# Half gate products over all 64 heads, eight steps of a bound one stage earlier, and the two norms around the second block rebuilt

## What is computed

```python
x = rms_norm(x_first, final_g)                    # x_first: the first block's rows
h = _rms(x, norm1_g_2)
u, q, k, v, qi, ki, wi, gates = split(h @ w_in_2)
y_ssm = s5(u); y_ssm = y_ssm * sigmoid(y_ssm @ w_glu + b_glu)     # gated unit
iscore = sum_h relu(qi_h . ki) * wi_h             # causal; 4 index heads
idx = top_k(iscore, 256)                          # per query row
y_att = softmax(q . k over idx) @ v               # 8 heads of 64, 8 blocks of 128 queries
merged = sigmoid(g_ssm) * (y_ssm @ w_proj_ssm) + sigmoid(g_att) * (y_att @ w_proj_attn)
x = x + merged @ w_out
h2 = _rms(x, norm2_g_2)
x = x + (silu(h2 @ w_gate) * (h2 @ w_up)) @ w_down
```

## Time and profile before

| | us |
|---|---|
| median of 3 runs | 3938.29 |
| lowest, highest | 3937.95, 3939.74 |
| the profiled execution | 3939.54 |
| its span in the profile | 3937.70 |

### The profile page before, as it was taken

How to read it: one execution, slowest core, us unless ns; L and a number is a source line. 1 busy time by engine, 2 the same in 40 slices (tenths; PEclk the granted TensorE clock), 3 DMA queues, 4 the chain that set the end, 5 groups by cost and what they waited for, 6 DMA issues and landing times. The chain is left out here.

```text
span 3937.7 us, 32752 instructions
## 1 busy us (share of the span) xinstructions
PE 3623.9 (92%) x12692; PEld 1910.6 (49%) x12692; DVE 1520.3 (39%) x2703; ACT 759.4 (19%) x1408; POOL 368.3 (9%) x347
## 2 busy tenths in 40 slices
PE   7998999987889499999987999889999899999999
PEld 3445656544765344444433664345544444444444
DVE  3526662576333400001008563978521322222420
ACT  2004451442431000000002223223220111111000
POOL 0000000014620000000001020000000122221000
PEclk8999998988989699999988999889999999999999
DMA  6400000014332598888844032112132111110300
GB/s 241 142 9 23 1 1 14 30 58 120 87 124 96 176 347 311 316 318 322 309 154 186 0 64 83 51 30 75 33 112 96 43 43 43 43 50 30 144 22 32
DMA packets 200718, 431.22 MB, mean 110 GB/s; under 512 B 71561, under 2 KB 125993, under 8 KB 187761
## 3 DMA queue, kind: packets, MB, share of 16 engines
q1 hardware_dynamic: 191154, 397.85, 29.2%
q0 software_dynamic: 8272, 29.38, 2.5%
q10 hardware_dynamic: 1152, 2.10, 0.1%
HBM read 380.04 MB, written 48.07 MB: 109 GB/s over the span
## 5 line engine op out<-in xcount | busy, mean ns | idle before, releaser
L1820 PE MATMUL psum<-arena 128*128 128x512 f32 x1536 | 673.1, 596 | 5.5 <-DMA arena<-in_w_gate_dram 3.1
L3165 PE MATMUL psum<-arena 128*128 128x512 f32 x1232 | 531.5, 594 | 5.7 <-DVE arena L3223 4.1
L1820 PEld LDWEIGHTS psum<-arena 128*128 128x128 f32 x1536 | 290.4, 191 | 365.5 <-issue 362.5
L3165 PEld LDWEIGHTS psum<-arena 128*128 128x128 f32 x1232 | 234.4, 191 | 302.2 <-issue 294.5
L3319 PE MATMUL psum<-arena 128*128 128x512 f32 x528 | 228.6, 595 | 3.6 <-PEq L3138 3.6
L2809 PE MATMUL psum<-arena 128*128 128x512 f32 x416 | 201.7, 629 | 0.1
L742 PE MATMUL psum<-arena 128*128 128x512 f32 (+1 forms) x512 | 198.2, 543 | 1.1 <-PEq L456 1.1
L2897 DVE TENSOR_SCALAR_CACHE_REDUCE arena<-arena 128x1024 f32<-128x1024 f32 (+2 forms) x192 | 173.7, 943 | 1.9
L477 PE MATMUL psum<-arena 64*128 64x512 f32 (+1 forms) x384 | 156.1, 551 | 11.1 <-ACT arena L531 10.2
L3319 PEld LDWEIGHTS psum<-arena 128*128 128x128 f32 x528 | 100.3, 190 | 132.0 <-issue 131.8
L2113 PE MATMUL psum<-arena 128*128 128x512 f32 (+1 forms) x384 | 162.1, 582 | 0.0
(11 more groups left out here) (514 smaller groups left out, 4674.2 us busy)
## 6 DMA issues: line engine op xcount, KB each, us to landing
arena<-in_w_gate_dram SPq DMA_DIRECT2D x32, 2048.0 KB, 7.4
arena<-in_w_up_dram SPq DMA_DIRECT2D x32, 2048.0 KB, 9.1
arena<-in_w_down_dram SPq DMA_DIRECT2D x32, 2048.0 KB, 8.0
arena<-in_w_mod_dram SPq DMA_DIRECT2D x12, 2048.0 KB, 9.5
arena<-gd_rows SPq DMA_DIRECT2D x56, 256.0 KB, 4.3
arena<-in_w_in_dram SPq DMA_DIRECT2D x22, 512.0 KB, 4.3
arena<-in_w_ffn_gate_dram SPq DMA_DIRECT2D x11, 1024.0 KB, 5.4
arena<-in_w_ffn_up_dram SPq DMA_DIRECT2D x11, 1024.0 KB, 5.4
```

The costliest lines, as they stand in the source:

```text
L1820: ins = nc.tensor.matmul(ps[:, banks + j, :], lhs[:, k], W[n][:, h, k % 4, j * 512:(j + 1) * 512], start=(k == 0), stop=(k == KD - 1))
L3165: ins = nc.tensor.matmul(out(q), left[:, k], right[:, k], start=first and k == 0, stop=last and k == 3, skip_group_check=not first)
```

## The change

- *Experts' stage.* `final_g` and `norm1_g_2` are both broadcast into rows of `e.rows` that are no longer used, and GpSimd, after its first two gathers, makes from them the product of the two gains and the square of the final gain.
- *Between the blocks.* GpSimd has no work. ScalarE squares a tile, keeping the squares (`x2`) and their sum; VectorE multiplies them by the squared gain and sums (`tensor_tensor_reduce`). The factors take six small steps. One scaling by the product of the gains gives `xn`; the residual rows are neither computed nor stored, and only their factors are kept (`e.r3`). All copies of the turned rows are ScalarE's, in an order written out by hand. The gain is no longer loaded here.
- *Gated unit's stage.* Ahead of each of the eight products, VectorE does one of the first eight units of pair (7,6).
- *Sparse stage.* It starts that pair at unit 8 and spreads the 25 units left over heads 0 to 15. The 52 half gate products are spread over all 64 heads; ScalarE's copies go with them.
- *Output stage.* Two tiles in flight, in four banks; the other four banks take transpositions. Tile t-2 is turned right behind the products of tile t, and each tile has its own factor and root. VectorE makes the residual from `x_dram`, the kept factor and the final gain.

```diff
@@ stage_experts, SyncE and GpSimd
-            sp.dma_start(e.fgain, broadcast_rows(e.in_["final_g"])).then_inc(e.s_fgain, 16)
+            sp.dma_start(e.rows[:, 1], broadcast_rows(e.in_["final_g"])).then_inc(s_fgain, 16)
+            sp.dma_start(e.rows[:, 2], broadcast_rows(e.in_["norm1_g_2"][0])).then_inc(s_fgain, 16)
...
             gather(0)
             gather(1)
+            pool.wait_ge(s_fgain, 32)
+            nc.gpsimd.tensor_tensor(e.rows[:, 2], e.rows[:, 2], e.rows[:, 1], ALU.mult).then_inc(e.s_gains, 1)
+            pool.wait_ge(e.s_gains, 1)
+            nc.gpsimd.tensor_tensor(e.rows[:, 1], e.rows[:, 1], e.rows[:, 1], ALU.mult).then_inc(e.s_gains, 1)
@@ stage_between, ScalarE
+                nc.scalar.activation(x2[:, t % 4], x[:, t], ACT.Square, scale=D ** -0.5, accum_out=ss[:, 0, t:t + 1]).then_inc(s_sq, 1)
...
+            for t in range(4):
+                squares(t)
+            root(0)
+            squares(4)
+            turned(0)
+            turned(1)
+            root(1)
+            squares(5)
+            squares(6)
...
@@ stage_between, VectorE
+            dve.wait_ge(e.s_gains, 2)
+            sum_with_gain(0)
+            sum_with_gain(1)
+            for i in range(TL // 2):
+                spread(i)
+                if i < TL // 2 - 1:
+                    sum_with_gain(2 * i + 2)
+                scaled(2 * i)
+                scaled(2 * i + 1)
+                if i < TL // 2 - 1:
+                    sum_with_gain(2 * i + 3)
@@
+BOUND_UNITS, UNITS_GLU = 33, 8
+def bound_unit(nc, step, tiles, scores, u):
+    cand, drop, count, _, *junk = tiles
+    if u == 0:
+        step(nc.vector.memset(cand.bitcast(F32), 0.0))
+    for j, b in enumerate(scores):
+        ins = nc.vector.tensor_scalar(junk[j][:, 0:b.shape[-1]], b, cand.bitcast(F32)[:, j:j + 1], 0.0, ALU.is_ge, ALU.add, accum_out=count[:, j:j + 1])
...
@@ stage_glu, VectorE
-            outputs(0, 4)
+            for u in range(4):
+                bound_unit(nc, step, e.bound, widest, u)
+                outputs(u, u + 1)
             scores(0, NI)
-            outputs(4, 8)
+            for u in range(4, 8):
+                bound_unit(nc, step, e.bound, widest, u)
+                outputs(u, u + 1)
@@ stage_sparse
+    halves = lambda n: [divmod(k, 2) for k in range(2 * GN * n // len(heads), 2 * GN * (n + 1) // len(heads))]
...
-                if n // 2 < GN:
-                    gates(n // 2, n % 2)
+                for q, half in halves(n):
+                    gates(q, half)
...
-            r = 0
+            r = UNITS_GLU
...
+                upto = UNITS_GLU + (BOUND_UNITS - UNITS_GLU) * (n + 1) // (2 * HEADS) if a < 2 else BOUND_UNITS * (n + 1) // (2 * HEADS)
+                while r < min(upto, BOUND_UNITS * len(pairs)):
@@ stage_out2, TensorE
+                if t >= 2:
+                    pe.wait_ge(s_x4, t - 1)
...
+                if t >= 2:
+                    turn(t - 2)
+            turn(TL - 2)
+            turn(TL - 1)
@@ stage_out2, ScalarE
+            for t in range(TL):
+                squares(t)
+                root(t)
+                if t >= 2:
+                    turned(t - 2)
+            turned(TL - 2)
+            turned(TL - 1)
@@ stage_out2, VectorE
+                nc.vector.scalar_tensor_tensor(out=e.x4[:, t], in0=xr[:, t % 2], scalar=e.r3[:, t:t + 1], in1=g[:, 0], op0=ALU.mult, op1=ALU.mult).then_inc(s_x3, 1)
...
+            for t in range(TL):
+                residual(t)
+                spread(t)
+                modulated(t)
```

More of the change, by code:

```diff
@@ L1917, in _ @@
                 output(i, False)
-    A.give(*("w_" + n for n in names), "xe", "xT", "sg", "hid", "hidT", "y", "gcol", "rows", "idxT", "gateT")
+    A.give(*("w_" + n for n in names), "xe", "xT", "sg", "hid", "hidT", "y", "gcol", "idxT", "gateT")
 def stage_between(e):
@@ L1934, in stage_between @@
     vv = A.take("vv", 2, TL)
+    rr = e.scale1.rearrange("p a b -> p (a b)").rearrange("p (a b) -> p a b", b=TL)
+    e.r3 = rr[:, 0]
+    gain_sq, gains = e.rows[:, 1], e.rows[:, 2]
     s_x = [e.sem(f"bt_xin{i}") for i in range(TL)]
     e.w_p2, e.s_wp2 = A.take("w_p2", 3, KD, 512, high=True), [e.keep_sem(f"p2_w{i}") for i in range(3)]
-    s_in, s_own, s_sq, s_sg, s_xg, s_var, s_rt, s_x3, s_n, s_tr, s_ev, s_ev2 = (
-        e.sem(f"bt_{n}") for n in ("in", "own", "sq", "sg", "xg", "var", "rt", "x3", "n", "tr", "ev", "ev2"))
+    s_own, s_sq, s_s1, s_var, s_rt, s_n, s_tr, s_ev = (e.sem(f"bt_{n}") for n in ("own", "sq", "s1", "var", "rt", "n", "tr", "ev"))
     e.s_hst = e.keep_sem("bt_hst")
-    s_st = [e.sem(f"bt_st{i}") for i in range(TL)]
-    NP = TL // 2
     with nc.Block() as block:
@@ L2002, in _, with sum_with_gain, spread @@
             step = Steps(dve, s_own)
[L2003 to L2007, removed]
+            def sum_with_gain(t):
+                dve.wait_ge(s_sq, t + 1)
+                if t >= 2:
+                    dve.wait_ge(s_s1, t - 1)
+                nc.vector.tensor_tensor_reduce(out=junk[:, t % 2], in0=x2[:, t % 4], in1=gain_sq, scale=1.0, scalar=0.0, op0=ALU.mult, op1=ALU.add,
+                                               accum_out=ss[:, 1, t:t + 1]).then_inc(s_s1, 1)
+            def spread(i):
                 c = slice(2 * i, 2 * i + 2)
-                dve.wait_ge(s_sg, 2 * i + 2)
-                step(nc.vector.tensor_scalar(ss[:, :, c], ss[:, :, c], 1.0 / D, None, ALU.mult))
+                dve.wait_ge(s_s1, 2 * i + 2)
                 step(nc.vector.tensor_scalar(vv[:, 0, c], ss[:, 0, c], EPS, None, ALU.add))
@@ L2016, in _, with scaled @@
                 nc.vector.tensor_tensor(vv[:, 1, c], vv[:, 1, c], vv[:, 0, c], ALU.mult).then_inc(s_var, 1)
[L2017 to L2028, removed]
-                    turned(2 * i - 2)
-                    turned(2 * i - 1)
-            turned(TL - 2)
-            turned(TL - 1)
+            def scaled(t):
+                dve.wait_ge(s_rt, t // 2 + 1)
+                dve.wait_ge(s_x[t], 16)
+                if t >= 2:
+                    dve.wait_ge(s_tr, 2 * (t - 1))
+                nc.vector.scalar_tensor_tensor(out=xn[:, t % 2], in0=x[:, t], scalar=rr[:, 1, t:t + 1], in1=gains, op0=ALU.mult, op1=ALU.mult).then_inc(s_n, 1)
+            dve.wait_ge(e.s_gains, 2)
[9 more added lines that the diff above has]
+                    sum_with_gain(2 * i + 3)
         @block.tensor
@@ L2044, in _ @@
                         ins.then_inc(s_tr, 1)
-    A.give("x", "xn", "gain1", "final_gain", "junk", "ss", "xg", "vv")
+    A.give("x", "xn", "x2", "junk", "ss", "vv", "rows")
 TWO_PI = 2 * np.pi
@@ L2637, in stage_glu @@
     rel = A.take("rel", 2, 512)
+    cand, drop = A.take("cand", 2).bitcast(I32), A.take("drop", 2).bitcast(I32)
+    e.bound = (cand, drop, A.take("count", 2), A.take("room", 2), A.take("rank", L), A.take("equal", L))
+    widest = [B(i) for i in e.chosen[::-1][0:2]]
     QI, KI = 4, 7
@@ L2747, in stage_sparse @@
     B = lambda i: e.bias[i]
-    equal, rank = A.take("equal", L), A.take("rank", L)
-    cand = A.take("cand", 2).bitcast(I32)
-    bound, drop = cand.bitcast(F32), A.take("drop", 2).bitcast(I32)
-    count, room = A.take("count", 2), A.take("room", 2)
     e.w_proj, e.s_wproj = A.take("w_proj", 2, 4, D, high=True), [e.keep_sem(f"mg_p{i}") for i in range(2)]
@@ L2761, in stage_sparse @@
     turns = free + chosen[::-1]
-    pairs = [chosen[::-1][i:i + 2] for i in range(0, len(chosen), 2)]
+    pairs = [[B(i) for i in chosen[::-1][k:k + 2]] for k in range(0, len(chosen), 2)]
     s_own, s_sel, s_bias = (e.sem(f"sp_{n}") for n in ("own", "sel", "bias"))
@@ L2880, in _ @@
                     softmax(n)
-                if n >= 2 and n % 2 == 0 and n // 2 <= GN:
-                    gates((n - 2) // 2)
+                for q, half in halves(n - 1) if n else ():
+                    if half:
+                        gates(q)
                 if n > HEADS and n % HEADS == 2:
@@ L3037, in stage_out2 @@
     xr = A.take("x_ring", 2, D)
-    g = A.take("gain", D)
+    g = A.take("gain", 2, D)
     h = A.take("h", 2, D)
@@ L3042, in stage_out2 @@
     s_x = [e.sem(f"o2_xin{i}") for i in range(2)]
[L3043 removed]
+    s_g = [e.sem(f"o2_g{i}") for i in range(2)]
+    s_mm, s_x3, s_x4, s_sq, s_var, s_rt, s_own, s_h, s_tr, s_ev = (e.sem(f"o2_{n}") for n in ("mm", "x3", "x4", "sq", "var", "rt", "own", "h", "tr", "ev"))
     two = lambda v: v.rearrange("p (a n) -> p a n", a=2)
```

193 lines of the change are left out of this document (86 added, 107 removed).

## The result

| | before | changed |
|---|---|---|
| median, us | 3938.12 (6 runs, 3936.96 to 3940.26) | 3911.10 (6 runs, 3906.37 to 3915.55) |
| the profiled execution | 3939.54 | 3910.64 |
| its span | 3937.7 | 3908.8 |

The ratio is 0.9931, 95% interval 0.9918 to 0.9943: faster by 27 us. The forecast was 3909.4, and the sum against the profiled execution (-28.9) is what was measured (-28.9). That agreement is partly luck, as the windows of the changed kernel show at once (us, busy us of PE, PEld, DVE, ACT, POOL, then clock, DMA share, GB/s). They answer to the earlier trace rows.

A forecast was written before the change was run, and what follows sets the result against it. VectorE was taken to pace the sparse stage's first regime, TensorE its second, with a VectorE, ScalarE and GpSimd chain between the blocks; -13.4 + 1.5 - 12.8 - 4.2 = -28.9 gave 3909.4 us, range 3901 to 3918.

The forecast's parts named there:

- Part 1, first scaling, -9.7: Between the blocks: without GpSimd's work, the first scaling starts at 2073.1, not 2082.8, saving 9.7 us.
- pace, -2.1: Between the blocks: VectorE sets the pace at 6.2 us a pair; three pairs take 18.6, not 20.7, saving 2.1 us.
- tail, -1.6: Between the blocks: from the last pair's start to the next stage takes 6.0 us, not 7.6, saving 1.6 us.
- Part 1, experts, +1.5: Experts' stage: one more 512 KB broadcast ahead of the gate weights, which TensorE awaits, costs 1.5 us.
- Part 2, -22.4 + 0.2: Eight bound steps leaving the sparse stage's VectorE-paced regime save 22.4 us; in the gated unit's stage they cost 0.2.
- It can: Sparse stage, heads 0 to 15: TensorE can follow when head 16 starts 90.7 us after head 0, not 113.1.
- Part 3, net +9.4: Sparse stage: spreading the half products over 64 heads costs net 9.4 us, as three halves return where TensorE sets the pace.
- Heads 16 to 51: 7 x 3.43 = -24.0: Sparse stage: these heads have 29 half products in place of 36, each worth 3.43 us, saving 24.0 us.
- slower: the heads without a half product let the clock fall: Sparse stage rival: nine heads after head 15 without a half product cost 5.4 us each, giving 3958; chance 0.04.
- Clock over the shorter pause: Rival: TensorE's clock stays up before head 16, giving 3904; chance 0.12, shared with spreading being free.
- Part 4, -4.2: Output stage: transpositions between products cost 6 us, the tail falls from 17.1 to 6.9; net saving 4.2 us.
- The rule on transpositions: Output stage: if transpositions don't count as clock work, the next stage's first matmuls cost 3.7 us more, giving 3912.9.

The follow-up runs named there:

- pool_beside: Changed kernel with GpSimd doing eight products between the blocks again, into memory nobody reads: 3924.46 us, ratio 0.9969.
- sparse_only: Kernel before with only the bound's eight units in the gated unit's stage and half products over 64 heads; norms as before: 3934.39 us, ratio 0.9997.
- no_steps: Changed kernel with the bound's eight steps back in the sparse stage, 33 units over heads 0 to 15: 3928.73 us, ratio 0.9978.
- no_spread: Changed kernel with one half product on each of heads 0 to 51 and none behind: 3893.68 us, ratio 0.9897.
- norms_only: Kernel before with only both norms and the gains' products changed; sparse stage and gated unit's as before: 3909.13 us, ratio 0.9930.
- shifted: Changed kernel with the same spreading, its phase moved: heads without a half product are 2, 7, 12, 18, 23, 28, 34 and on: 3903.45 us, ratio 0.9914.

## Why the prediction was right, and where it was not

- **Part 1, first scaling, -9.7; pace, -2.1; tail, -1.6.** Right in place and size. From the load's issue to the first scaling it is 10.3 us, before 20.0; the three pairs take 17.5 (forecast 18.6, before 20.7); from the last pair on it is 5.7 (forecast 6.0). The sum is -15.0 for -13.4. The terms held the order of the chain and the slow steps together; pool_beside shows that work beside the chain is enough to undo nearly all of it.
- **Part 1, experts, +1.5.** Wrong: 0. TensorE's wait for the gate weights was 2.23 us, not 3.09 + 1.5; it was 0.64 to 2.48 in the other kernels with the broadcast and 2.49 in sparse_only, without it. That answers to the earlier trace rows. Of all traces only that of the kernel before has 3.09, and only its matmuls take 596 ns in the mean; this is the -5.5 of the table.
- **Part 2, -22.4 + 0.2.** The step that a unit costs 2.79 is right, and so is the cover in the gated unit's stage: a step and a product take 3.39 us there (2400.24 to 2403.63 in the changed kernel), with no wait of VectorE behind the first, which answers to the earlier trace rows. But by VectorE's lines, as in the earlier trace rows, head 16 starts 93.7 us after head 0 (2443.73 to 2537.40), not 90.7. The failed step is "It can", of TensorE: VectorE waited 3.51 us for it at head 8, where the kernel before has no such wait; the clock is 0.83 over that regime and a half product of 3.70 us takes up to 6.4. By the medians Part 2 is worth 17.6 and 15.4. With the spreading the sparse stage gives 17.4 of it (434.2 to 416.8). Without it that stage gives 20.1 (415.5 to 395.4), while the gated unit's goes from 46.6 to 50.1 at a lower clock (0.99 and 0.92); that isn't the steps' doing, since it takes 49.9 in no_steps, which has none there.
- **Part 3, net +9.4.** The mis-sized term, and the cause of the sparse stage's miss: +21.4. "Heads 16 to 51: 7 x 3.43 = -24.0" holds for five heads of the seven. For heads 16 and 32 it took for granted that TensorE is fast and sets the pace there. The rival *slower: the heads without a half product let the clock fall* had this mechanism and drew its line at six heads of nine; it came true at two, and at one of these, head 16, the clock was already down. The ten halves at the end cost 31.2 (33.1 forecast), and the merge behind them is shorter by 0.4 us (sparse_only against before) to 2.9 (changed against no_spread), a term the sum did not have.
- **Clock over the shorter pause.** The pause was 9.84 us (forecast some 10) and the clock fell, so that rival is out.
- **Part 4, -4.2.** -3.7, and -6.1 in norms_only. From the first product to the end of the last it is 116.0 us (110.1 + 6), and the tail is 7.5 (6.9) for 17.1. The same stage takes 121.1 to 123.6 us from trace to trace, so the half microsecond to the forecast says nothing.
- **The rule on transpositions.** Of the Trainium skill, "TensorE: Matmul & The Clock Gate", Part 4: PE-mode transpose, the forecast said that the trace disagrees. The rows of the changed kernel that answer to the earlier trace rows are:

```profile
3088.11 1.91 PE L3083 MATMUL psum<-arena 128*128 128x128 f32 x16
3092.78 1.90 PE L3083 MATMUL psum<-arena 128*128 128x128 f32 x8 [2.76 <-DVE arena L3148]
3095.62 7.43 PE L3207 MATMUL psum<-arena 128*128 128x512 f32 x12 [0.94 <-PEq L3057]
```

After a wait of 2.76 us the last eight transpositions run at 0.24 us each and the twelve records behind them at 0.62, so the clock was down, as that page's rule would have it, and as the wait alone would too: no run here parts the two. In no_spread the same wait is followed by fast transpositions, and only the products behind them are slow (the clock is 0.56 from 3075.10 to 3079.00):

```profile
3073.10 1.09 PE L3083 MATMUL psum<-arena 128*128 128x128 f32 x8 [2.76 <-DVE arena L3148]
3075.19 7.05 PE L3207 MATMUL psum<-arena 128*128 128x512 f32 x12 [0.99 <-PEq L3057]
```

Against the rule stands the kernel before: under transpositions alone its clock goes from 0.50 (3112.50 to 3114.50) to 1.00 (3116.00 to 3120.00). The fall in the changed kernel cost 0.8 us in the transpositions and none in the next stage, where the second large run of products starts 11.5 us after the first product in both kernels. The 3.7 us worked out from the rule were not there (and 3909.4 + 3.7 is 3913.1, not 3912.9).

Two of the forecast's own signs of being right did not come: head 16 started 93.7 us after head 0 and not 90 to 92, and from head 16 to the end the stage took 19.9 us longer, not some 9. One sign of being wrong did come, a wait of VectorE for TensorE in the first 16 heads. So the total came out by luck: the 13 us missing in the sparse stage were made up by the stretch between the blocks, which gave more than forecast, and by stages to which the forecast gave nothing, some of which the change doesn't touch. Besides the experts' matmuls, the scan's stage takes 117.3 to 121.1 us and the gated unit's 46.6 to 51.1 from trace to trace. In the latter it is the clock: 0.87 over the stage in the kernel before, 0.91 in the changed one, 0.99 in norms_only. The forecast had no term for that: its parts were read from one execution.

## What to carry to other kernels

Work for an idle engine pays only where it is idle: filler products belong into the pauses that another engine makes (two of them there were worth 8.6 us), and taking one from a stretch where it hid that engine's work gave nothing back and cost some us more. Ask of each place what stands behind it when the filler is gone, and give the first piece behind a pause the densest work. Before giving GpSimd a product beside a chain on VectorE, read VectorE's smallest instructions in that window. And compare a stage's duration over several traces before a difference of 1% in one of them is called a gain.

## What the hardware showed that was not expected

- **TensorE's clock can fall behind short waits, but the length of the wait doesn't settle it.** In the traces shown, waits of 1.46, 2.29, 2.36 and 2.76 us were each followed by work at 1.2 GHz; waits of 0.45 and, once, 1.42 were not, and neither was the 2.38 us ahead of the output stage in the kernel before, behind which 256 records take 110.11 us, 0.43 each. Behind 1.46 in shifted and behind 2.76 in no_spread the first transpositions are still fast, and only what follows is slow. What else decides is not shown.
- **What stands behind a pause sets its price.** Behind the pause before head 16 the clock was 0.50 over the next 20 us in the changed kernel, where head 16 has no product; in no_spread, where it has one, it was 0.80 over the same stretch.
- **A step on 128x2 waits for GpSimd.** Beside GpSimd's products of 2.3 to 2.8 us, VectorE's small steps take 2.06 to 2.27 us, all but the reciprocals, which keep 0.17; once GpSimd is done, all take 0.17.
- **It goes both ways.** GpSimd's eight products took 18.47 us in the kernel before and 22.48 in pool_beside, where VectorE has more large passes beside them. That these passes are the cause was not tried by itself.
